# A float32 encoder layer with hierarchical experts on one core: output projection's first operands moved ahead of a stage barrier

## The reference, cut to what matters

```python
mod = silu(c) @ w_mod + b_mod                      # shift, scale, gate, twice
h = modulate(rms_norm(x, norm1), sh1, sc1)
q, k, v, fl, xb, gb = split(h @ w_in)
o_a = fox_attention(q, k, v, log_sigmoid(fl + b_f))
o_b = rglru_branch(xb, gb)
g_a, g_b = split(sigmoid(h @ w_gate + b_gate))
mix = g_a * (o_a @ w_pa) + g_b * (o_b @ w_pb)
x = x + g1 * (mix @ w_out)
h2 = modulate(rms_norm(x, norm2), sh2, sc2)
x = x + g2 * hier_moe(h2)        # 4 groups of 8 experts, the best 2 experts of the best group
y = rms_norm(x, norm_f)
```

## Time and profile before

| | |
|---|---|
| median of 3 runs | 2208.09 us (2206.21 to 2212.84) |
| the profiled execution | 2206.62 us, its span 2205.0 us |
| instructions | 30360 |
| TensorE busy | 2020.1 us (92%), weight loads 1732.3 us |
| VectorE, ScalarE, GpSimd busy | 1341.0, 1070.6, 355.7 us |
| mean granted TensorE clock | 0.963 of full |
| DMA | 415.95 MB, mean 189 GB/s |

### The profile page before, as it was taken

How to read it: one execution, slowest core, us unless ns; L and a number is a source line. 1 busy time by engine, 2 the same in 40 slices (tenths; PEclk the granted TensorE clock), 3 DMA queues, 4 the chain that set the end, 5 groups by cost and what they waited for, 6 DMA issues and landing times. The chain is left out here.

```text
span 2205.0 us, 30360 instructions
## 1 busy us (share of the span) xinstructions
PE 2020.1 (92%) x11833; PEld 1732.3 (79%) x11833; DVE 1341.0 (61%) x1790; ACT 1070.6 (49%) x1401; POOL 355.7 (16%) x275
## 2 busy tenths in 40 slices
PE   5998999999988999999999999699799999999970
PEld 2887777777755899999999999587688888888860
DVE  3523565555564255565453443477699888888868
ACT  3422343443344255564343332312578777778754
POOL 1000000000001221230110001232113222222200
PEclk8999999999998899999999999899899999999995
DMA  7313111114288211125454484434799999999956
GB/s 253 103 60 100 59 59 59 50 55 129 87 257 280 75 41 39 31 78 163 137 167 141 137 231 128 145 109 169 279 378 377 375 376 390 398 379 390 386 216 257
DMA packets 247460, 415.95 MB, mean 189 GB/s; under 512 B 23687, under 2 KB 187143, under 8 KB 221730
## 3 DMA queue, kind: packets, MB, share of 16 engines
q1 hardware_dynamic: 234402, 383.23, 50.4%
q0 software_dynamic: 11008, 24.20, 2.9%
q10 hardware_dynamic: 1920, 6.70, 0.8%
HBM read 382.65 MB, written 45.66 MB: 194 GB/s over the span
## 5 line engine op out<-in xcount | busy, mean ns | idle before, releaser
L386 DVE TENSOR_TENSOR ew_lo<-region,ew_hi 128x2048 fp32r<-128x2048 f32 x192 | 432.2, 2285 | 26.8 <-ACT ew_hi L2154 26.0
L2154 ACT ACTIVATE ew_hi<-region 128x2048 fp32r<-128x2048 f32 x192 | 368.0, 1918 | 114.8 <-DMA region<-in_w 113.1
L386 DVE TENSOR_TENSOR wm_lo<-weights,wm_hi 128x1024 fp32r<-128x1024 f32 x91 | 125.2, 1378 | 159.3 <-ACT wm_hi L1283 158.6
L2642 PE MATMUL PS<-ew_lo,xT_hi 128*128 128x512 f32 x512 | 203.5, 398 | 6.2 <-issue 5.7
L2644 PE MATMUL PS<-ew_hi,xT_hi 128*128 128x512 f32 x512 | 201.0, 393 | 0.0
L2643 PE MATMUL PS<-ew_hi,xT_lo 128*128 128x512 f32 x512 | 200.4, 391 | 0.0
L1427 DVE CUSTOM_DVE_ANT_0 region<-PS,region 128x896 f32<-128x896 f32 (+7 forms) x128 | 91.9, 755 | 145.8 <-PE PS L1668 145.8
L1283 ACT ACTIVATE wm_hi<-weights 128x1024 fp32r<-128x1024 f32 x92 | 97.1, 1057 | 141.7 <-DMA weights<-in_w_pa 78.7
L1161 ACT ACTIVATE region<-region,small 128x896 f32<-128x896 f32 (+7 forms) x128 | 98.8, 772 | 119.0 <-DVE small L1427 119.0
L393 PE MATMUL PS<-h_lo,wx_hi 128*128 128x384 f32 x384 | 133.7, 348 | 2.9 <-POOL wx_lo L386 2.9
L394 PE MATMUL PS<-h_hi,wx_lo 128*128 128x384 f32 x384 | 129.4, 337 | 0.0
(11 more groups left out here) (402 smaller groups left out, 4828.7 us busy)
## 6 DMA issues: line engine op xcount, KB each, us to landing
region<-in_w SPq DMA_DIRECT2D x192, 1024.0 KB, 7.8
weights<-in_w_gate SPq DMA_DIRECT2D x46, 512.0 KB, 3.9
region<-in_w_mod SPq DMA_DIRECT2D x20, 1024.0 KB, 5.6
weights<-in_w_in SPq DMA_DIRECT2D x36, 512.0 KB, 4.0
weights<-in_w_pb SPq DMA_DIRECT2D x24, 512.0 KB, 3.6
weights<-in_w_pa SPq DMA_DIRECT2D x24, 512.0 KB, 3.5
region<-F_d SPq DMA_DIRECT2D x16, 512.0 KB, 6.4
weights<-in_cache_k SPq DMA_DIRECT2D x8, 1024.0 KB, 7.9
```

What stands on the lines that cost most here:

```text
L386: return eng.tensor_tensor(lo, x, hi.bitcast(F32), ALU.subtract)
L2154: act(ewh[u], ew[u], ACT.Copy).then_inc(sem(f"eu_hi{u}"), 1)
L2642: mm(out, lh(c), ewl[u][:, c, :], start=first and c == 0, stop=False)
```

## The change

- In mixing, ScalarE and VectorE also split wo[0], in four pieces of two chunks (`wo_first`: at ob 19, oa 19, ob 20, oa 20), and the tiles mt[0] and mt[1] (`mt_first`: at ob 22 and oa 22). SyncE loads these two tiles and the router's weights and biases in steps 20 and 21, and wo[1] after the last panel.
- ob 22 and oa 22 use the gate slots 2 and 3 instead of 0 and 1.
- The last sum, chunk 23, is made by VectorE, and SyncE stores it (mix_st_last). No engine waits for the last stores before the barrier: mix_st0, mix_st_last and wo1_in are kept out of the clearing and are waited for in block 3 (tile 6; ScalarE's split of wo[1]). GpSimd then clears the rest in four ranges, not one.
- Buffers move, so that all this has room: wo and its parts, the tiles and their parts, h2, norm2, x1b, the experts' high parts.
- G2's 8 sample rows and norm_f are loaded with G2 at the first expert. Units 4 and 5 of expert 0 wait for the last router products (`lg_mm`), no longer for h2's stores.

```diff
-        def clear_semaphores():
+        def clear_semaphores(*kept):
             nc.all_engine_barrier()
-            nc.clear_and_free_semaphores(list(sems.values()))
+            nc.clear_and_free_semaphores([v for k, v in sems.items() if k not in kept])
             nc.all_engine_barrier()
...
-        mix_slot = [first_slots[k] if k < 2 * LEAD else {"ob": 0, "oa": 1, "gate": 2 + q}[kind] for k, (kind, x, q) in enumerate(mix_order)]
+        mix_slot = [first_slots[k] if k < 2 * LEAD else {"ob": 2 * (x == XS - 2), "oa": 1 + 2 * (x == XS - 2), "gate": 2 + q}[kind] for k, (kind, x, q) in enumerate(mix_order)]
...
+        wo_first = {k: 2 * n for n, k in enumerate(k for k, what in enumerate(mix_order) if what[0] != "gate" and what[1] in (XS - 5, XS - 4))}
+        mt_first = {k: n for n, k in enumerate(k for k, what in enumerate(mix_order) if what[1] == XS - 2 and what[0] != "gate")}
...
+                    if x == 2 * CH + 4:
+                        e.wait_ge(*panel_used(mix_place["ob", 2 * CH - 1, 1]))
+                        for j in range(2):
+                            e.wait_ge(sem(f"mix_st{j}"), CH // 2 * 16)
+                        for j in range(2):
+                            e.dma_start(mt[j], mix_tile(j * P)).then_inc(sem(f"mt_first{j}"), 16)
+                        e.dma_start(wr[:, :, 0:GR], a["w_rg"][0].rearrange("(c p) n -> p c n", p=P)).then_inc(sem("wr_in"), 16)
+                    if x == 2 * CH + 5:
+                        e.dma_start(wr[:, :, GR:], a["w_re"][0].rearrange("(c p) n -> p c n", p=P)).then_inc(sem("wr_in"), 16)
+                        e.dma_start(br[:, 0:GR], spread(a["b_rg"])).then_inc(sem("wr_in"), 16)
+                        e.dma_start(br[:, GR:], spread(a["b_re"])).then_inc(sem("wr_in"), 16)
+                e.wait_ge(*panel_used(mix_place["gate", XS - 1, 1]))
+                e.dma_start(wo[1], w_out[:, :, 512:1024]).then_inc(sem("wo1_in"), 16)
+                e.wait_ge(sem("early_in"), 3 * MOD_LOAD)
+                e.wait_ge(sem("wr_in"), 64)
+                e.wait_ge(sem("mix_last"), 1)
+                e.dma_start(mix_d[(CH - 1) * P:CH * P, 2 * NG:3 * NG], tm[1][0]).then_inc(sem("mix_st_last"), 16)
...
-                for j in range(2):
-                    e.wait_ge(sem(f"mix_st{j}"), G3 * CH // 2 * 16)
...
+                e.wait_ge(sem("mixp"), XS)
+                e.wait_ge(sem("mixd1"), XS // 2)
+                tt(tm[1][0], tm[1][0], tm[1][1], ALU.add).then_inc(sem("mix_last"), 1)
...
-        clear_semaphores()
+        clear_semaphores("mix_st0", "mix_st_last", "wo1_in")
...
-                e.wait_ge(sem("ht_mm0"), PT_ // 2 + 2)
-                e.wait_ge(sem("ht_mm1"), PT_ // 2)
-                e.wait_ge(sem("h2_out0"), 16 * (PT_ // 2 + 1))
-                e.wait_ge(sem("h2_out1"), 16 * (PT_ // 2))
+                e.wait_ge(sem("lg_mm1"), PT_ // 2)
+                e.wait_ge(sem("lg_mm0"), PT_ // 2 + 1)
                 for s in range(NE):
                     if s == 0:
                         load_units(slice(s, s + 1), s, (4, 5))
-                        e.dma_start(G2[0], spread(mod_d[0:1, 5 * D:6 * D])).then_inc(sem("g2_in"), 16)
+                        mod_load(e, G2, 5, "g2_in")
+                        e.dma_start(NF, spread(a["norm_f"].rearrange("(a d) -> a d", a=1))).then_inc(sem("g2_in"), 16)
```

More of the change, by code:

```diff
@@ L72, in sem @@
             return sems[name]
-        def clear_semaphores():
+        def clear_semaphores(*kept):
             nc.all_engine_barrier()
-            nc.clear_and_free_semaphores(list(sems.values()))
+            nc.clear_and_free_semaphores([v for k, v in sems.items() if k not in kept])
             nc.all_engine_barrier()
-            sems.clear()
+            for k in [k for k in sems if k not in kept]:
+                del sems[k]
         at = {}
@@ L282, in panel_used, with columns @@
             return sem(f"wm_mm{mix_slot[k]}"), mix_turn[k] + 1
-        wo = [view(R2, 0, CH, TOK)[:, :, 0:512], view(R4, 4096, CH, 512)]
-        woh = [part(f"wo_hi{k}", "weights", 4096 * k, CH, 512) for k in range(2)]
-        wol = [part(f"wo_lo{k}", "region4", 4096 * k, CH, 512) for k in range(2)]
+        def columns(whole, off, width=P):
+            return whole[:, :, off:off + width]
+        wo = [columns(view(R2, 0, CH, TOK), 512 * k, 512) for k in range(2)]
+        wol = [columns(hTl, 512 * k, 512) for k in range(2)]
+        woh = [columns(obl, 0, 512), part("wo_hi1", "weights", 4096, CH, 512)]
         def pieces(chunk, off, width):
@@ L292, in trunk @@
         B2, xo = [pieces(4 * k, 512, 256) for k in range(2)], [pieces(4 * (1 - k), 768, 256) for k in range(2)]
[L293 to L297, removed]
+        mt = [columns(obT, 512 + P * j) for j in range(2)]
+        mtl = [columns(obl, 512 + P * j) for j in range(2)]
+        mth = [columns(hTl, D), columns(hTh, D)]
+        h2 = [view(WR, D * j, D) for j in range(2)]
+        h2T = [columns(obT, 768 + P * j) for j in range(2)]
+        junk, N2 = view(WR, 2 * D, D), view(WR, 3 * D, D)
         ssq_a, bias_b = small[:, 40:41], small[:, 41:42]
@@ L1034, in _ @@
                     if x == 2 * CH:
[L1035 removed]
+                        e.dma_start(wo[0], w_out[:, :, 0:512]).then_inc(sem("wo0_in"), 16)
                         e.wait_ge(sem("mod_st"), 16 * 8)
@@ L1972, in load_units @@
                         e.dma_start(ew[u], unit_of(ex_id, u)).then_inc(sem(f"eu_in{u}"), 16)
[L1973 to L1976, removed]
-                e.dma_start(NF, spread(a["norm_f"].rearrange("(a d) -> a d", a=1))).then_inc(sem("g2_in"), 16)
                 e.wait_ge(sem("h2_made1"), PT_ // 2)
@@ L2534, in half @@
                     for c in chunks:
-                        if first and c % 2 == 0:
-                            e.wait_ge(sem("wo_lo"), k * 4 + c // 2 + 1)
+                        if first and k and c % 2 == 0:
+                            e.wait_ge(sem("wo_lo"), c // 2 + 1)
                         mm(out, mth[j][:, c, :], wol[k][:, c, :], start=c == 0, stop=False)
```

94 lines of the change are left out of this document (48 added, 46 removed).

## The result

| | before | changed |
|---|---|---|
| first comparison, median of 6 runs each | 2207.76 us (2206.21 to 2212.84) | 2198.03 us (2189.88 to 2201.05) |
| ratio of the two, 95% interval | | 0.9949 (0.9933 to 0.9966) |
| profiled execution | 2206.62 us, span 2205.0 | 2199.07 us, span 2197.4 |
| TensorE busy, granted clock over the span | 2020.1 us, 0.963 | 2017.9 us, 0.966 |

The kernel became faster by 0.51%, 9.7 us (by the interval 7.5 to 14.8); forecast were 15.0. There it gained 15.7 and 17.2 us. So the first comparison stands at the low end of what the change is worth, and the first question is why.

The account below looks back on a forecast made before the run. TensorE, busy 2020.1 of 2205.0 us, was taken as the bound, with time to win only in its waits and low clock. -3.1 - 12.6 + 0.2 + 0.5 = -15.0 gave a median of 2193.1 us, range 2187.5 to 2199.5.

Parts of the forecast that it names:

- Part 1: Step 22 of mixing: new slots remove the waits of 1.69 and 1.44 us, -3.13 us; oa 21's 1.80 stays.
- part 4: Mixing: the added copies, subtractions and sum cost 0; SyncE's added loads share the DMA queue with oa 21, +0.2 us.
- Part 2: Hole before the projection: 4.3 us instead of 16.95, -12.6 us, with +0.8 for three more clears and drains.
- Part 3: Block 3: w_out's second half, still split there, and the loads of norm2 and x are not late; cost 0.
- Part 5: Start of the experts: 1 MB more loaded there, units 4 and 5 earlier; +0.5 us, between 0 and 2.6.
- the 3 us that were named as a sign of being wrong: First gather: the prediction is wrong if TensorE's wait there grows by over 3 us.
- Part 6: Clock after the hole: the same low-clock stretch of some 14 matmuls follows; 0, between -2.8 and 0 us.
- Rival A: After the short hole the clock does not fall or rises at once: 2190.5 us, or 2188.8; chance 0.13.
- Rival C: Mixing: SyncE gets stuck issuing small router pieces, ob 22 comes late, +2.3 us, 2195 to 2196; chance 0.09.
- D: Projection's first four halves: the clock stays low, each matmul costs 0.20 us more, up to 2214.3 us; chance 0.03.
- B: Hole before the projection: the barrier waits for the store after all, +4.5 us, 2197.6 us; chance 0.08.
- Rival E: First gather: the saved time is waited for there, full 2.6 us plus a clock dip, 2198 us; chance 0.05.

Follow-up runs that it names:

- a_wait_stores: The changed kernel with SyncE waiting for the last two stores of mixing before the barrier; TensorE's wait at the projection grew by 1.5 us.
- a_pool_last: The changed kernel with the last sum and its store on GpSimd again, not waited for at the barrier; TensorE's wait was 8.2 us against 4.4.
- a_swap24: The changed kernel with the second and fourth large buffers exchanged in SBUF, addresses alone; 2193.92 us, against 2194.01 for the changed kernel beside it.

## Why the prediction was right or wrong

Forecast were 2193.1 us in a range of 2187.5 to 2199.5; the first comparison gave 2198.03, the two later ones 2194.0 and 2194.3 with a kernel before that stood 2 to 4 us higher than in the first. Faster was right. The forecast of 15.0 us lies below the gain of both later comparisons (15.7, 17.2) and above that of the first (9.7), just outside its interval.

- *Part 1, slots: right, a little small.* ob 22, oa 22 and oa 23 have no wait. That of oa 21 stayed, as said, at 2.1 us instead of 1.8: its split on ScalarE began 3.90 us after the issue (1359.46 from 1355.56), not 3.57, which is the +0.2 of part 4.
- *Part 2, the hole: right in sum, wrong in one mechanism.* 4.4 us for a forecast of 4.3. The sum on VectorE took its 0.56. The clears cost 0.5 instead of 0.8. What failed is the reading of the 5.3 us between GpSimd's store and the barrier: the text took them for the store's landing, and said that the trace did not agree with the 2.5 us that it had estimated by the Trainium skill, *DMA: Bandwidth & Descriptors*, section "Anatomy of one DMA". For the landing the trace does agree, roughly: 2.1 us in the DMA view. The other 3.1 us are GpSimd's drain (2.68) and the steps to the barrier, and the rows of line 866 show this without any experiment. The forecast came out because the change removed both at once. The gain of a change that only dropped the wait would have been forecast 3.7 us too high.
- *Part 3: right.* No wait for w_out's right half in the list of waits.
- *Part 4, insertions: right.* 0.3 us at oa 21. Not foreseen, and without cost: four of GpSimd's sums of 0.98 us take 1.9 beside VectorE's new pieces.
- *Part 5, the experts' start: the term that was mis-sized.* +0.5 was forecast, +2.9 in the profiled run, just below the 3 us that were named as a sign of being wrong, and +1.0 in the three further traces of the changed kernel (8.2 against 7.1; with the first trace, 10.1, the mean is +1.5). The prediction saw both halves, the 1 MB and the earlier units, and netted them by guess; the runs show the units' share (wait 7.2 to 6.05 when nothing follows them) and the price of what follows (2.1).
- *Part 6, clock: half wrong.* The clock fell, as forecast, but for eight matmuls and not fourteen. The fourteen were themselves one draw: the steps of 0.39 us or more between the projection's first matmuls number 13, 8 and 12 in the three traces like before, and 7, 8, 10 and 7 in the four of the changed kernel. From the projection's first matmul to its first transposes it takes 23.5 to 24.0 us in the changed kernel, and 23.8 to 24.5 before: 0.6 us less in the mean. Rival A, with no low clock at all, did not come.
- *Rival C* is out: wr's first part took SyncE 1.89 us and the larger one 0.58, where it took 3.80 with the full queue. So the 3.80 were the queue's. *D* is out, with the clock at 1.00 from 1394 to 1500. *B* is out for SyncE by `a_wait_stores`; for GpSimd `a_pool_last` shows just such a drain behind a running store, and the change escaped it by giving the store to SyncE.
- *Rival E* has the place right (the first gather) and was given 0.05. In the first comparison the time came out at E's 2198, but not by E: three further traces have 1 us there. In the profiled run the rest was the experts' draw; of the five other runs there is no trace.
- What the prediction lacked altogether is how far one execution may lie from another. It had three times of before, 2206.21 to 2212.84, and allowed a run 1 to 2 us. Seventeen runs spread over 16 us. Its range was wide enough because of its rivals, and not because it knew this.

## What to carry to other kernels

Cut two traces at a few fixed points of the program before you explain a difference of the whole: 15.5 us were gained exactly where forecast, and what seemed lost later was mostly two single draws of a loop bound by transfers, seen only with a dozen traces. Where an engine is late at a barrier, look for the drain at the end of its block and not only for the waits in the program: behind a store of 192 KB GpSimd came to the barrier 3.7 us after the issue, SyncE 0.7. And where a load is moved, look for the one small transfer on the path behind it: 1.5 MB that nobody needed for 620 us stood ahead of the gather that everybody waited for.

## What the runs showed of the hardware that was not expected

- GpSimd's drain at the end of a block waits for its own last store: in eleven traces it ended 1.2 to 1.4 us after the landing, which took 2.1 to 4.5 us. Started after the landing it still took 2.68 us (three traces like before). SyncE's drain behind the same store took 0.13 us.
- The gather of the first expert's tokens takes 6.0 us from the moment its slots are known to TensorE's start, 2.63 of them issue, when nothing is queued ahead of it (6.05, 6.0 and 6.1 in three kernels). What stands in the engines adds 1 to 4 us to it.
- SyncE's time to issue one and the same load depends on what is queued: 3.80 us behind more than 4 MB, 0.58 behind a panel.
- In the hole of 4.4 us of the changed kernel's first trace the granted clock stayed at 1.00. It fell to 0.50 only 0.9 us after TensorE had restarted, for 3.3 us. In `a_swap24`, with the same hole, it fell within the hole, and so it did in `a_wait_stores` with one of 5.9 us (0.69, then 0.50); in the hole of 17 us it was at 0.50 from 1390 on.
- GpSimd's addition of 128x384 took 0.98 us alone and 1.9 us while VectorE subtracted 128x1024 pieces beside it.
